# A two-layer attention trunk on one core: vector work reordered ahead of the gate, four projection banks, the first head turned by TensorE, a new filling of the last period

## The reference, cut to what matters

```python
for i in range(DEPTH):                      # 2 layers; x is (1, 512, 1024), 8 heads of 128
    hdn = rms_norm(x, norm_g[i])
    proj = hdn @ w_in                       # q, k, v and the gate's z, 4 x 1024 columns
    q, k, v, z = split(proj)
    q = rms_norm(split_heads(q), q_norm);  k = rms_norm(split_heads(k), k_norm)
    # layer 0: rotary tables on q and k; causal block-sparse attention, which for
    #          512 tokens in two blocks of 256 with one earlier block is full causal attention
    # layer 1: no rotary; scores get c[q] - c[k], c the running sum of log_sigmoid(forget logits)
    p = softmax(masked(q @ k.T * d**-0.5 [+ bias]))
    y = merge_heads(p @ v) * silu(z)
    x = x + y @ w_out[i]
```

## Time and profile before

| | us |
|---|---|
| median of 3 runs | 563.06 (562.56 to 564.03) |
| the profiled execution, its own time | 564.51 |
| its span (first to last instruction) | 562.5 |
| PE busy in the span | 545.7 (97%) |
| DVE, POOL, ACT busy | 408.6, 294.1, 286.6 |

### The profile page before, as it was taken

The page is one execution under the profiler, slowest core; times in us unless marked ns, Lnnn a source line. Parts: engine busy times, 40 slices in busy tenths (PEclk is TensorE's granted clock), DMA queues, the critical chain, the costliest instruction groups (busy, mean ns, idle before and its releaser), DMA issues.

```text
span 562.5 us, 9740 instructions
## 1 busy us (share of the span) xinstructions
PE 545.7 (97%) x2958; PEld 499.9 (89%) x2958; DVE 408.6 (73%) x1039; ACT 286.6 (51%) x841; POOL 294.1 (52%) x348
## 2 busy tenths in 40 slices
PE   6998999999999999999999989999999999999998
PEld 4997999999999999878888989999999999998887
DVE  3799797979797979774363767787869595959321
ACT  5735555555454546453445463736464647373500
POOL 4854545454544444425545576657475756663700
PEclk9999999999999999999999999999999999999999
DMA  9812323131313131204442334423341535141221
GB/s 280 215 49 87 93 58 95 56 95 56 93 56 93 56 93 56 93 8 130 108 102 76 95 90 80 95 76 79 90 112 56 118 50 131 37 131 37 76 93 57
DMA packets 78237, 49.95 MB, mean 89 GB/s; under 512 B 4089, under 2 KB 71417, under 8 KB 78210
## 3 DMA queue, kind: packets, MB, share of 16 engines
q1 hardware_dynamic: 78208, 49.61, 32.6%
q10 hardware_dynamic: 2, 0.00, 0.0%
HBM read 47.48 MB, written 2.11 MB: 88 GB/s over the span
## 4 chain that ended last, share of the span: by engine, by line
PE 52%; DVE 17%; POOL 12%; issue 12%; ACT 3%; DMA 2%; SPq 1%; POOLq 0%; ACTq 0%; DVEq 0%
PE banks L343 14%; PE banks L345 14%; PE banks L344 14%; DVE banks L853 11%; POOL w_lo L1064 8%; PE banks L458 3%; POOL rstd L1082 3%; DVE pT_lo L894 2%; PE banks L444 2%; PE banks L375 1%; DMA w_raw<-in_b_w_in_dram 1%; POOL msq L1080 1%; DMA first_raw<-in_a_w_in_dram 1%; ACT junk L626 1%; PE banks L433 1%
## 5 line engine op out<-in xcount | busy, mean ns | idle before, releaser
L1064 POOL TENSOR_TENSOR w_lo<-w_raw,w_hi 128x512 fp32r<-128x512 f32 x147 | 188.4, 1300 | 94.8 <-ACT w_hi L590 94.8
L343 PE MATMUL banks<-w_hi,hT_hi 128*128 128x384 f32 x512 | 175.2, 342 | 8.7 <-DVE qkn L842 4.6
L345 PE MATMUL banks<-w_hi,hT_lo 128*128 128x384 f32 x512 | 172.2, 336 | 0.0
L344 PE MATMUL banks<-w_lo,hT_hi 128*128 128x384 f32 x512 | 172.2, 336 | 0.0
L853 DVE STREAM_TRANSPOSE banks<-qkn 32x256 f32<-32x256 f32 x256 | 116.6, 456 | 3.5
L343 PEld LDWEIGHTS banks<-w_hi,hT_hi 128*128 128x128 f32 x512 | 96.8, 189 | 13.1 <-DVE qkn L842 7.3
L590 ACT ACTIVATE w_hi<-w_raw 128x512 fp32r<-128x512 f32 x148 | 87.8, 643 | 21.8 <-DMA w_raw<-in_b_w_in_dram 13.9
L344 PEld LDWEIGHTS banks<-w_lo,hT_hi 128*128 128x128 f32 x512 | 97.0, 189 | 0.7
L345 PEld LDWEIGHTS banks<-w_hi,hT_lo 128*128 128x128 f32 x512 | 96.8, 189 | 0.0
L1080 POOL TENSOR_TENSOR msq<-ssq,eps 128x2 f32<-128x2 f32 x64 | 13.9, 218 | 125.0 <-ACT junk L626 125.0
L919 DVE RECIPROCAL gz<-gz 128x128 f32<-128x128 f32 x64 | 58.1, 928 | 0.0
(11 more groups left out here) (108 smaller groups left out, 877.5 us busy)
## 6 DMA issues: line engine op xcount, KB each, us to landing
w_raw<-in_b_w_in_dram SPq DMA_DIRECT2D x64, 256.0 KB, 4.0
w_raw<-in_a_w_in_dram SPq DMA_DIRECT2D x52, 256.0 KB, 2.9
w_raw<-in_w_out_dram SPq DMA_DIRECT2D x32, 256.0 KB, 2.9
first_raw<-in_a_w_in_dram SPq DMA_DIRECT2D x12, 256.0 KB, 5.6
cos_t<-c_rows SPq DMA_DIRECT2D x8, 256.0 KB, 3.7
out_dram<-xs SPq DMA_DIRECT2D x7, 256.0 KB, 2.0
xs<-in_x_dram SPq DMA_DIRECT2D x3, 512.0 KB, 5.8
xs<-in_x_dram SPq DMA_DIRECT2D x2, 256.0 KB, 2.9
```

The costliest lines, as they stand in the source:

```text
L343: pe.matmul(dst, ah, bh, start=first and m == 0, stop=False)
L344: pe.matmul(dst, ah, bl, start=False, stop=False)
L345: mm = pe.matmul(dst, al, bh, start=False, stop=last and m == n - 1)
L1064: pool.tensor_tensor(w_lo[:, slot, k, :], raw, f32(w_hi[:, slot, k, :]), ALU.subtract).then_inc(wlo_set, by)
```

## The change

What it does, part by part:

- Projection tiles get four banks, 0, 1, 6 and 7, and `ssq` and `rstd` four entries. PE's `qkv`, ACT's `read_qkv` and POOL's `rstd_qk` of a tile now wait for the same tile of the head before (`a - TILES + 1` in place of `a - 1`). Turned q and k move to banks 4 and 5.
- DVE's period: norm of tile 0, maxima, norm of tile 1 and the reciprocals of the sums stand ahead of `low_y` and of the gate's four reciprocals, which follow in a row.
- ACT's and POOL's period: squares and roots of tile 1 stand ahead of weight chunk 1, the exponentials ahead of chunk 2; on POOL chunks 1 to 3 stand ahead of the root of tile 2, and 4 and 5 ahead of that of tile 3.
- Layer 0's first head is turned by eight PE transposes (`turn_first_qk`) after its `zproj`, not by DVE.
- `last`: eleven chunk products ahead of the scores instead of eight, ACT's first four weight chunks ahead of the exponentials, and five to eight chunk products of output unit (1, 0), now in bank 7, between `values` and the rest.

```diff
-        ssq = sb("ssq", [P, 2, 2])
+        ssq = sb("ssq", [P, TILES, 2])
         msq = sb("msq", [P, 2, 2])
-        rstd = sb("rstd", [P, 2, 2])
+        rstd = sb("rstd", [P, TILES, 2])
...
-        Z_BANK, Y_BANK, QT_BANK = 2, 3, 6
+        Z_BANK, Y_BANK, QT_BANK, SPARE_BANK = 2, 3, 4, 6
...
-            return (0, 1, 3, 4)[t] if layer == 0 and isinstance(h, int) and h == 0 else t % 2
+            return (0, 1, 3, 4)[t] if layer == 0 and isinstance(h, int) and h == 0 else (0, 1, 6, 7)[t]
...
-            return 3 if layer == 0 and t == 1 else QT_BANK
+            if layer == 1:
+                return QT_BANK
+            return 3 if t == 1 else SPARE_BANK
 
         def unit_bank(c, t):
 
-            return QT_BANK if c == 0 and t == 3 else t
+            return {(0, 3): SPARE_BANK, (1, 0): SPARE_BANK + 1}.get((c, t), t)
...
-                wait(pe, qkn_set, a - 1)
+                wait(pe, qkn_set, a - TILES + 1)
...
+            def turn_first_qk():
+
+                pe.wait_ge(qkn_set, TILES)
+                for m in range(2):
+                    for t in range(TILES):
+                        mm = pe.transpose(banks[:, QT_BANK + m, t * P:(t + 1) * P], qkn[:, t, m, :], ident[:, :])
+                mm.then_inc(qk_turned, 1)
...
+                if layer == 0:
+                    turn_first_qk()
...
                 project(layer, 0, 0, range(6), True, False)
-                project(layer, 0, 1, range(2), True, False)
+                project(layer, 0, 1, range(5), True, False)
                 scores(layer, h, 1)
-                project(layer, 0, 1, range(2, 6), False, False)
+                project(layer, 0, 1, [5], False, False)
                 pe.wait_ge(ylo_set, g - 1)
-                project(layer, 0, 0, [6], False, False)
-                project(layer, 0, 1, [6], False, False)
-                project(layer, 0, 3, range(5), True, False)
+                for t in range(2):
+                    project(layer, 0, t, [6], False, False)
+                project(layer, 0, 3, range(7), True, False)
+                pe.wait_ge(gate_set, g)
+                project(layer, 0, 2, [0], True, False)
                 turn_probs(layer, h)
-                project(layer, 0, 3, range(5, 7), False, False)
-                pe.wait_ge(gate_set, g)
-                project(layer, 0, 2, range(3), True, False)
+                project(layer, 0, 2, range(1, 6), False, False)
                 values(layer, h, 1)
-                project(layer, 0, 2, range(3, 7), False, False)
+                project(layer, 0, 2, [6], False, False)
+                pe.wait_ge(wlo_set, KC * (JOBS * layer + HEADS + 2))
+                project(layer, 1, 0, range(5), True, False)
                 pe.wait_ge(ylo_set, g)
                 for t in range(TILES):
                     project(layer, 0, t, [h], False, True)
-                pe.wait_ge(wlo_set, KC * (JOBS * layer + HEADS + 2))
-                for t in range(TILES):
+                project(layer, 1, 0, range(5, HEADS), False, True)
+                for t in range(1, TILES):
                     pe.wait_ge(x_added, u + 1 + t)
                     if layer + 1 == LAYERS and t == TILES - 1:
                         for part in out_parts[-2:]:
                             project_part(*part)
                     else:
                         project(layer, 1, t, range(HEADS), True, True)
...
-                split_w(layer, h + 2, s, (0, 1, 2))
+                split_w(layer, h + 2, s, (0,))
                 read_qkv(layer, h + 1, 1 - s, 1)
+                split_w(layer, h + 2, s, (1,))
                 exps(layer, h)
+                split_w(layer, h + 2, s, (2,))
+                normalise(layer, h)
                 split_w(layer, h + 2, s, (3,))
-                normalise(layer, h)
-                split_w(layer, h + 2, s, (4,))
                 read_qkv(layer, h + 1, 1 - s, 2)
-                split_w(layer, h + 2, s, (5,))
+                split_w(layer, h + 2, s, (4, 5))
                 read_qkv(layer, h + 1, 1 - s, 3)
                 split_probs(layer, h)
                 split_w(layer, h + 2, s, (6, 7))
...
+                split_w(layer, h + 2, 1, (0, 1, 2, 3))
                 exps(layer, h)
                 normalise(layer, h)
-                split_w(layer, h + 2, 1, (0, 1, 2, 3, 4))
+                split_w(layer, h + 2, 1, (4, 5))
                 split_probs(layer, h)
-                split_w(layer, h + 2, 1, (5, 6, 7))
+                split_w(layer, h + 2, 1, (6, 7))
...
+                wait(dve, pTlo_set, 3 * g)
...
-                turn_qk(layer, 0)
+                    turn_qk(layer, 0)
...
-                late = not isinstance(h, int) or h > 0
-                if late:
+                if not isinstance(h, int) or h > 0:
                     gate_y(layer, h - 1)
                 split_qk(layer, h)
-                if late:
+
+            def late_y(layer, h):
+                if not isinstance(h, int) or h > 0:
                     low_y(layer, h - 1)
 
             def period(layer, h, s):
                 begin(layer, h)
-                silu_part(layer, h, 0)
-                silu_part(layer, h, 1)
                 split_v(layer, h + 1, 1 - s, 0)
                 norm_qk(layer, h + 1, 0)
-                silu_part(layer, h, 2)
                 maxima(layer, h)
                 split_v(layer, h + 1, 1 - s, 1)
                 norm_qk(layer, h + 1, 1)
                 invert_sums(layer, h)
-                silu_part(layer, h, 3)
+                late_y(layer, h)
+                for n in range(4):
+                    silu_part(layer, h, n)
...
                 begin(layer, h)
-                silu_part(layer, h, 0)
+                late_y(layer, h)
+                for n in range(2):
+                    silu_part(layer, h, n)
                 maxima(layer, h)
-                silu_part(layer, h, 1)
                 invert_sums(layer, h)
...
                 rstd_qk(layer, h + 1, 0)
                 if layer == 1 and isinstance(h, int):
                     mask_bias(h)
-                split_w(layer, h + 2, s, (0, 1, 2))
+                split_w(layer, h + 2, s, (0,))
                 rstd_qk(layer, h + 1, 1)
-                split_w(layer, h + 2, s, (3, 4))
+                split_w(layer, h + 2, s, (1, 2, 3))
                 rstd_qk(layer, h + 1, 2)
-                split_w(layer, h + 2, s, (5,))
+                split_w(layer, h + 2, s, (4, 5))
                 rstd_qk(layer, h + 1, 3)
                 split_w(layer, h + 2, s, (6, 7))
```

More of the change, by code:

```diff
@@ L211, in build_trunk @@
         out_parts += [(bank, t, slice(cols.start, cols.start + CH // 2)),
-                      (QT_BANK, t, slice(cols.start + CH // 2, cols.stop))]
+                      (SPARE_BANK, t, slice(cols.start + CH // 2, cols.stop))]
         sin_flat = sin_t[:, :, :, :].rearrange("p a b n -> p (a b n)")
@@ L564, in last @@
                         project(layer, 1, t, range(HEADS), True, True)
-                    if layer + 1 < LAYERS and t >= 1:
+                    if layer + 1 < LAYERS:
                         turn_hidden(layer + 1, t - 1)
@@ L622, in read_qkv @@
                 act.wait_ge(a_done, a + 1)
-                wait(act, rstd_set, a - 1)
+                wait(act, rstd_set, a - TILES + 1)
                 wait(act, ssq_set, a)
@@ L626, in read_qkv @@
                     sq = act.activation(junk[:, m, :], banks[:, qkv_bank(layer, h, t), m * P:(m + 1) * P],
-                                        ACT.Square, scale=SCALE, accum_out=ssq[:, t % 2, m:m + 1])
+                                        ACT.Square, scale=SCALE, accum_out=ssq[:, t, m:m + 1])
                 sq.then_inc(ssq_set, 1)
@@ L825, in norm_qk @@
                         last = dve.scalar_tensor_tensor(out=qkn[:, t, m, :], in0=banks[:, qkv_bank(layer, h, t), m * P:(m + 1) * P],
-                                                        scalar=rstd[:, t % 2, m:m + 1], in1=cos_t[:, 0, m, :],
+                                                        scalar=rstd[:, t, m:m + 1], in1=cos_t[:, 0, m, :],
                                                         op0=ALU.mult, op1=ALU.mult)
@@ L832, in norm_qk @@
                     dve.scalar_tensor_tensor(out=rot[:, t % 2, m].rearrange("p (a n) -> p a n", a=2), in0=swapped,
-                                             scalar=rstd[:, t % 2, m:m + 1],
+                                             scalar=rstd[:, t, m:m + 1],
                                              in1=sin_t[:, t, m].rearrange("p (a n) -> p a n", a=2),
@@ L838, in norm_qk @@
                     part = banks[:, qkv_bank(layer, h, t), m * P:(m + 1) * P]
-                    dve.scalar_tensor_tensor(out=part, in0=part, scalar=rstd[:, t % 2, m:m + 1], in1=cos_t[:, t, m],
+                    dve.scalar_tensor_tensor(out=part, in0=part, scalar=rstd[:, t, m:m + 1], in1=cos_t[:, t, m],
                                              op0=ALU.mult, op1=ALU.mult).then_inc(rot_set, 1)
@@ L1078, in rstd_qk @@
```

(6 more changed lines are left out.)

## The result

| | before | changed |
|---|---|---|
| median | 563.20 (562.56 to 564.03, 4 runs) | 556.38 (556.16 to 556.99, 4 runs) |
| profiled execution, and its span | 564.51, 562.5 | 556.99, 555.2 |

What follows compares the result with a forecast made beforehand. PE was taken to bound the kernel, with layer 0's periods held by a chain through DVE. Gains of 6.0, 2.0 and 3.7 sum to 11.7 us, from 563.06 to 551.4 us, range 549.0 to 555.5.

Steps and rivals of the forecast that it cites:

- The chain that was to bind in layer 0: Layer 0: DVE's cycle, its last norm behind two weight chunks on POOL, at 27.6 us over PE's 27.07.
- the 1.7 us of lowered clock: Layer 1's head 0: PE's clock averages 0.72 over 6.00 us behind the 1.97 us wait; 1.7 us counted as gain.
- The last periods: Layer 0's head 7 and the stretch after: waits of 1.69 and 0.47 us go, less some restart; gain 2.0, ends 1.0 and 2.2.
- layer 0: Layer 0 to the start of head 7: from 198.7 to 192.7 us, gain 6.0.
- layer 1's head 0: Layer 1's first head: the 1.97 us wait and 1.7 us of lowered clock go, gain 3.7; the gate is late next.
- DVE's cycle in layer 0, after: Layer 0's period on DVE: maxima 1.7 us earlier, last norm at +16.9 instead of +17.39, cycle 28.08 to 27.6 us.
- First head turned by PE: Layer 0's head 0: transposes cost 1.0 us, the 1.58 wait goes, DVE starts about 2.5 us earlier; later waits total 2.2.
- `low_y` and the gate: Layer 0's period: gate ready at +13.6 or +14.1, `zproj` due about +14.2; cover 0.6 or 0.1 us, sum unchanged.
- Rival (c): Layer 1's head 0: the lowered clock was the profiled execution's own, absent from ordinary runs; 553.1 us, chance 0.13.
- (a): Layer 0: DVE's cycle hides fully behind PE, another 2.2 us gained, 549.2 us; chance 0.12.
- (b): Layer 0: DVE's cycle does not shrink, POOL's second chunk costs all the maxima gain, 554.3 us; chance 0.16.
- (d): Weight loads in layer 1's periods: late landings of 10.2 us make seven periods each wait 1.9, slower at 565; chance 0.03.

Runs made afterwards that it cites:

- four banks alone: The kernel before with only the four projection banks, their four entries and waits, every list as before: 562.62 us against 563.31, ratio 0.9987.
- `low_y` first: The changed kernel with `low_y` back right behind `split_qk`: 557.77 us, ratio 0.9886 to the kernel before.
- the holding experiment: The changed kernel with chunk 5 behind tile 3's root, layer 1's first chunks loaded early, and POOL waiting for x tile 0's norm before chunks 2 and 3: 550.80 us.
- The early loads: The changed kernel with chunk 5 behind tile 3's root, and SP issuing layer 1's first four weight chunks before the loads that wait for the last head's y: 551.27 us.
- chunk 5 behind the root: The changed kernel with POOL's weight chunk 5 moved behind the root of tile 3: 552.44 us, again 552.24.
- the second series: The changed kernel run again without edit: 555.69 us against 563.13 for the kernel before on that chip, ratio 0.9869.
- old filling: The changed kernel with the last period's order on PE, ACT and DVE as in the kernel before: 557.83 us, ratio 0.9898 to the kernel before.
- head 0 turned by DVE: The changed kernel with layer 0's first head turned by DVE as before, not by PE: 557.70 us, ratio 0.9895 to the kernel before.

## Why the prediction came out wrong

The chain that was to bind in layer 0 was right. What failed are terms of the sum: the 1.7 us of lowered clock, which most executions did not have; "The last periods", at 2.0 where 0.6 came; layer 0, at 6.0 where 4.85 came; and layer 1's head 0, where a wait that had been counted at nothing stayed.

**Layer 0, forecast 6.0, measured 4.85.** The mechanism was right: the last norm at +16.9 behind two chunks, PE waiting for `pT_lo`. Two sizes in "DVE's cycle in layer 0, after" and in "First head turned by PE" were off. First, "from the last norm to the next `gate_y` nothing changes": it went from 10.69 to 10.82 us, since the transposes now wait for `pT_lo` on the same engine (they start 1.64 after it, before 1.53). So the cycle is 27.72, not 27.6; over the five periods that show it this is 0.6. The kernel with four banks alone has the same 0.1. Second, the slack of "about 2.5 us": DVE's first `gate_y` stood 72.32 - 66.96 = 5.36 us behind the start of PE's work after `values`, against 5.74 in the steady state, which is 0.4 of slack and gone in one period. Turning by PE frees DVE early, but in its head-0 period DVE then waits 1.53 us for PE's scores and 1.39 for POOL's last root, so the end of the period does not hang on when it began. These are the rows:

```profile
66.96 0.19 PEld L345 LDWEIGHTS banks<-w_hi,hT_hi 128*128 128x128 f32 x1
```

```profile
72.32 0.69 DVE L919 TENSOR_TENSOR gz<-banks,gz 128x512 f32<-128x512 f32 x1
```

Over PE's floor stand 193.88 - 189.5 - 1.0 = 3.4 us, where 2.2 were counted.

**`low_y` and the gate: cover of 0.1 to 0.6 us.** `low_y` took 1.72, more than both rows named, the gate came at 169.30 - 155.49 + 0.69 = +14.5, and PE waited for it (0.49 by the weight loads). As the prediction had it, this wait is absorbed by the one for `pT_lo`: without it (`low_y` first) nothing is gained. The rule of the Trainium skill ("SBUF — State Buffer", section on the two separate sides) that these two exclude each other agrees with this trace, and the holding experiment shows it by removing only the overlap. What was mis-sized, at no cost to the sum, is the price, taken from the 1.16 of the earlier trace rows. There POOL's subtractions end at 259.09 + 2.55 = 261.64 and `low_y` at 261.02 + 1.16 = 262.18, 0.54 later. In the new place POOL's ends at 164.12 + 1.30 = 165.42 and `low_y` at 164.25 + 1.72 = 165.97, 0.55 later. So in both `low_y` ended some 0.55 us after the subtraction that it met, and the price is what was left of that: here nearly all of it, since `low_y` started 0.13 behind it.

**"The last periods", forecast 2.0, measured 0.6.** Two things failed. First, the size: 1.69 and 0.47 are the brackets of weight loads. PE's matmuls of the kernel before were idle for less:

```profile
243.46 0.50 PE L431 MATMUL banks<-qkT_hi 128*128 128x512 f32 x1 [1.26 <-DVE qkT_lo L860]
276.81 0.66 PE L375 MATMUL banks<-ident,qkn 128*128 128x128 f32 x4 [0.23 <-DVE qkn L784]
```

So some 1.5 us could be won, not 2.16. Second, the step "the 0.47 may go with it": it grew to 0.47 + 1.25, and in the matmuls of the changed kernel to

```profile
272.74 0.66 PE L377 MATMUL banks<-ident,qkn 128*128 128x128 f32 x4 [1.01 <-DVE qkn L800]
```

1.26 + 0.23 - 1.01 is 0.5, close to the measured 0.6. x tile 0 was complete some 5 us earlier (265.62 + 0.69, before 270.74 + 0.69), but the norm that PE waits for stands behind weight chunks that SP issues only after `low_y` of the last head, and that ended only 3.3 us earlier (261.02 + 1.16 in the earlier trace rows, 258.17 + 0.69 now). The early loads show this part, and holding POOL the other: the norm's 2.42 us contained 1.0 of contention in the kernel before too (2.45 there).

**"Layer 1's head 0", forecast 3.7, measured 3.19 in the profiles, and by estimate some 1.6 in the medians.** In the profiles the wait of 1.97 and the lowered clock are gone and a wait for `pT_lo` is new, 0.80 by the weight loads and 0.37 by the matmuls:

```profile
338.92 0.68 PE L468 MATMUL banks<-pT_hi,v_hi 128*128 128x512 f32 x2 [0.37 <-DVE pT_lo L911]
```

Without the clock's share, 1.97 - 0.37 = 1.6 is left. The prediction named the gate as next; it was the same pair of chunks ahead of tile 3's root, which it had priced for layer 0 alone and put at nothing here. POOL of the changed kernel there:

```profile
333.22 2.55 POOL L1082 TENSOR_TENSOR w_lo<-w_raw,w_hi 128x512 fp32r<-128x512 f32 x2
...
336.00 0.69 POOL L1100 TENSOR_TENSOR rstd<-msq,power 128x2 f32<-128x2 f32 x1
```

DVE's last norm waited 2.63 us for that root, and chunk 5 behind the root removes PE's wait. Rival (c) held: the lowered clock was that of the profiled execution and of about one in three others, and 1.5 to 1.7 us of the forecast gain were not in the median.

**The sum.** 11.7 less 1.15, 1.4, 0.5 and 1.7 is 7.0; the medians differ by 6.8 and, in the second series, 7.4. Of the rivals, (a) did not come (it took the edit of POOL's list to reach PE's floor), (b) did not (27.72, not 28.08), (c) did, and (d) did not: no weight's transfer holds PE in layer 1's periods. The range failed because the misses all had one sign, that of the last periods passed its own lower end (0.6, not 1.0), and the rival on the clock was kept apart from them.

## What to carry to other kernels

When several engines share a cycle, list what the last-arriving item waits for in each in-order queue, and look for an item in front of it that is not due: here one weight chunk moved behind a root was worth 3.5 us, half as much as the whole change. Take the size of PE's wait from its matmuls' rows, or from starts of work, and not from the idle of weight loads: that was 0.2 to 0.4 us too long in each of the places above. A term that rests on one lowered-clock stretch belongs in the sum only with the share of executions that show it. And a transfer whose wait guards something else (here the gain loads' wait, with weights queued behind it) should be looked for as soon as the wait in front of it moves.

## What was not expected of the hardware

- Operations of DVE with two inputs in SBUF that met a subtraction of POOL ended 0.54 to 0.55 us after it. `low_y` took 0.68 alone and 1.72 when it started 0.13 behind a subtraction of 1.30. The pair of norms took 1.42 alone, 2.42 beside one subtraction (it ended at 272.68, POOL's at 272.14) and 3.42 beside two (268.40 and 267.85, with the early loads). POOL's own took 1.49 to 1.65 there instead of 1.27 to 1.30.
- Idle stretches of PE's matmuls of 1.80 (old filling, head 7), 1.94 and 1.97 us, and a pair of 0.67 and 1.02 (head 0 turned by DVE), were each followed by a stretch at the lower clock level, some 3.4 us long; one of 1.86 (four banks alone, head 7) was not, nor was a pair of 0.65 and 1.02 (`low_y` first). In two thirds of the executions of the kernel before, the mean clock shows no such stretch.
- The first matmuls run at half pace, with a granted clock of 1.00 in the table by stretches, until 14.2 to 17.2 us into the span, differently in each execution. The start of z moves with it, from 31.9 to 33.6.
